# Two transformer blocks on one core: the second feed-forward begun with half of its second gate tile, kept in a place of its own, and the last input norm taken in two halves of the tokens

## What is computed

```
        x = x + rmsnorm(merged @ w_out[l], post_mix_w[l])
        h = rmsnorm(x, pre_ffn_w[l])
        f = (jax.nn.silu(h @ w_gate[l]) * (h @ w_up[l])) @ w_down[l]
        x = x + rmsnorm(f, post_ffn_w[l])
```

## Time and profile before

| | us |
|---|---|
| median of 3 runs | 2957.29 |
| lowest, highest | 2957.23, 2958.44 |
| the profiled execution, whole | 2958.75 |
| its span in the trace | 2956.9 |
| mean granted TensorE clock, as a share of 2.4 GHz | 0.991 |

### The profile page before, as it was taken

One profiled execution on the slowest core, in us unless ns is written; L12 is line 12 of the kernel. 1 busy time (PEld: TensorE's weight loads), 2 busy tenths in 40 slices (PEclk: granted clock), 3 DMA queues, 4 the chain that ended last, 5 costly groups with the idle time before them and its releaser, 6 DMA issues.

```text
span 2956.9 us, 31552 instructions
## 1 busy us (share of the span) xinstructions
PE 2868.3 (97%) x13108; PEld 2322.7 (79%) x13108; DVE 1393.5 (47%) x1660; ACT 957.4 (32%) x1255; POOL 369.7 (13%) x333
## 2 busy tenths in 40 slices
PE   8999999999999999999999999999999999999997
PEld 6877668888888888788878887667777888888886
DVE  6775544453535453633234444665564213232334
ACT  4313442321312122321246565654352222111122
POOL 1213112000000000201012222133320000000004
PEclk9999999999999999999999999999999999999998
DMA  3225523111111111245423332665531111111113
GB/s 116 79 79 137 145 65 109 49 39 61 42 52 40 61 36 54 93 142 185 162 72 98 107 93 78 192 203 167 210 118 56 41 57 39 61 36 58 43 61 118
DMA packets 88655, 270.01 MB, mean 91 GB/s; under 512 B 12600, under 2 KB 17336, under 8 KB 88512
## 3 DMA queue, kind: packets, MB, share of 16 engines
q1 hardware_dynamic: 74016, 221.61, 24.1%
q0 software_dynamic: 14496, 46.38, 4.5%
HBM read 215.35 MB, written 52.59 MB: 91 GB/s over the span
## 4 chain that ended last, share of the span: by engine, by line
PE 83%; DVE 8%; ACT 3%; issue 2%; DMA 2%; POOL 1%; DVEq 0%; SPq 0%; ACTq 0%; POOLq 0%
PE ps L211 82%; DVE cacc L182 1%; ACT PB L176 1%; PE ps L214 1%; POOL ga L179 1%; DVE PB L182 1%; DVE ps L191 1%; DVE YA L179 1%; DVE sqacc L179 1%; DVE YA L182 0%; DVE XT L179 0%; DMA xin<-in_xT 0%; DMA raw<-in_w_w2out 0%; ACT wh L176 0%; DVE AL L182 0%
## 5 line engine op out<-in xcount | busy, mean ns | idle before, releaser
L211 PE MATMUL ps<-AH,wh 128*128 128x512 f32 (+1 forms) x2232 | 887.5, 398 | 38.1 <-DVE wl L179 13.3
L211 PE MATMUL ps<-AH,wl 128*128 128x512 f32 (+1 forms) x2232 | 871.7, 391 | 0.0
L211 PE MATMUL ps<-AL,wh 128*128 128x512 f32 (+1 forms) x2232 | 871.2, 390 | 0.0
L179 DVE TENSOR_TENSOR wl<-raw,wh 128x1024 fp32r<-128x1024 f32 (+2 forms) x227 | 269.4, 1187 | 808.7 <-ACT wh L176 808.6
L211 PEld LDWEIGHTS ps<-AH,wh 128*128 128x128 f32 (+1 forms) x2232 | 418.8, 188 | 140.1 <-DVE AL L182 15.4
L176 ACT ACTIVATE wh<-raw 128x1024 fp32r<-128x1024 f32 (+2 forms) x274 | 252.5, 922 | 766.4 <-PE ps L211 754.2
L211 PEld LDWEIGHTS ps<-AH,wl 128*128 128x128 f32 (+1 forms) x2232 | 418.6, 188 | 91.1
L211 PEld LDWEIGHTS ps<-AL,wh 128*128 128x128 f32 (+1 forms) x2232 | 419.0, 188 | 88.3 <-issue 2.9
L211 PE MATMUL ps<-UH,wh 128*128 128x512 f32 (+1 forms) x840 | 325.2, 387 | 0.0
L211 PE MATMUL ps<-UL,wh 128*128 128x512 f32 (+1 forms) x840 | 325.1, 387 | 0.0
L211 PE MATMUL ps<-UH,wl 128*128 128x512 f32 (+1 forms) x840 | 325.1, 387 | 0.0
(11 more groups left out here) (219 smaller groups left out, 3209.0 us busy)
## 6 DMA issues: line engine op xcount, KB each, us to landing
raw<-in_w_up SPq DMA_DIRECT2D x44, 512.0 KB, 3.4
raw<-in_w_gu SPq DMA_DIRECT2D x44, 512.0 KB, 3.4
raw<-in_w_w2in SPq DMA_DIRECT2D x32, 512.0 KB, 4.3
raw<-in_w_down SPq DMA_DIRECT2D x48, 256.0 KB, 2.6
raw<-in_w_down SPq DMA_DIRECT2D x32, 320.0 KB, 2.8
xin<-in_xT SPq DMA_DIRECT2D x16, 512.0 KB, 4.8
stk<-scr_ka SPq DMA_DIRECT2D x32, 256.0 KB, 8.1
raw<-in_w_w2v SPq DMA_DIRECT2D x16, 512.0 KB, 3.4
```

Source lines behind the costliest of these rows:

```text
L179: return Issued(self, self.e.tensor_tensor(out, a, b, op))
L211: return Issued(self, self.e.matmul(out, l, r, start=start, stop=stop))
```

## The change

g1 is made early. Its two parts get a place of their own, slot 5 of `UH2` and `UL2`, which is free once the `w_out` product is over. The first half of g1 (bank 6) moves ahead of the second halves of g0 and u0. Norm 6 becomes two norms: 6 for the first 512 tokens, whose sums lie in u0's first half and whose rows lie in g1's first half, and 7 for the last 512, whose sums (bank 4 now) lie in g1's second half and whose rows lie in u1's first half. The sums and rows of norm 5 each move two values of k earlier. g0 and u0 are evacuated in halves (`first2`), u0's first half at the end of `dve_out2`. All later norms have a number one higher.

```diff
-    staged = [TILE["gu", ("g", 0)], TILE["gu", ("u", 0)]]
+    staged = [TILE["gu", ("g", 0)], TILE["gu", ("u", 0)], G1]
...
         elif s == staged[0]:
-            out += [(staged[0], 0), (staged[1], 0), (staged[0], 1), (staged[1], 1)]
-        elif s != staged[1]:
+            out += [(t, half) for half in range(2) for t in staged]
+        elif s not in staged:
...
     def w_halves(self, s):
+        if s == G1:
+            return self.UH2[:, 5, :], self.UL2[:, 5, :]
...
     def w_freed(self, q, s):
+        elif s == G1:
+            q.wait_ge(self.S.gem, GEM_END[TILE["w2out", (1, 7)]])
...
         def stats5(half, k):
-            if k == 6:
+            if k == 4:
                 q.wait_ge(S.pa, 21)
                 self.norm_stats(q, 5, self.acc3, 4, 8)
         def rows5(half, k):
-            if k == 2:
+            if k == 0:
                 self.norm_rows(q, 5, self.rcols[:, 12:16], 4, 8)
+            if k == 4:
+                q.wait_ge(S.xacc, 14)
+                self.norm_stats(q, 6, self.acc3, 0, 4)
+        def rows6(half, k):
+            if k == 4:
+                q.wait_ge(S.nrb, 4)
+                self.norm_rows(q, 6, self.rc8[:, 0:4], 0, 4)
...
         self.half_product(q, u0, self.Ah, self.Al, 8, 0, 2, P, None, None, True, True, rows5)
+        self.half_product(q, G1, self.Ah, self.Al, 8, 0, 6, P, None, None, True, True, rows6)
...
         x3(7, 0)
         self.norm_sqrt(q, 5, 4)
+        self.w_high(q, G1)
         rows(1)
+        self.norm_sqrt(q, 6, 4)
         for n in range(NT):
             x3(n, 1)
-        self.w_high(q, TILE["gu", ("g", 1)])
+            if n == 3:
+                q.wait_ge(S.nrow, 6)
+                q.act(self.RB[:, HALF[0]], self.bank(4), ACT.Copy).then_inc(S.nrb)
...
+    def first2(self, q, x, half):
+        q.wait_ge(self.S.gem, GEM[TILE["gu", ("g", 0)] + x, half])
+        q.wait_ge(self.S.nrb, 6 + half)
+        t = q.tt(self.cv2[2 * x][:, HALF[half]], self.bank(2 * x + half), self.RB[:, HALF[half]], ALU.mult)
+        t.then_inc(self.S.uev if half else self.S.fuh)
...
         self.w_low(q, TILE["gu", ("u", 0)])
+        self.norm_recip(q, 5, self.rcols[:, 12:16], 4)
         low(7, 0)
         total(0)
-        self.norm_recip(q, 5, self.rcols[:, 12:16], 4)
+        self.w_low(q, G1)
         mult(0, 1)
         mult(1, 1)
+        self.norm_recip(q, 6, self.rc8[:, 0:4], 4)
         add(0, 1)
...
+        self.first2(q, 1, 0)
         total(1)
-        self.w_low(q, TILE["gu", ("g", 1)])
...
+        q.wait_ge(S.nsq, 6)
+        self.half_product(q, G1, self.Ah, self.Al, 8, 1, 7, P, None, None, True, True, stats7)
+        q.wait_ge(S.fuh, 1)
+        self.half_product(q, G1 + 1, self.Ah, self.Al, 8, 0, 2, P, None, None, True, True, rows7)
+        self.f2_evac(q, 1)
+        self.half_product(q, G1 + 1, self.Ah, self.Al, 8, 1, 3)
...
         self.w_low(q, TILE["gu", ("u", 1)])
-        self.norm_recip(q, 6, self.rc8, 8)
-        evac(0)
-        evac(1)
+        self.first2(q, 0, 0)
+        self.norm_recip(q, 7, self.rc8[:, 4:8], 4)
+        self.first2(q, 0, 1)
+        self.first2(q, 1, 1)
+        gated(0)
```

More of the change, by code:

```diff
@@ L88 @@
 LAST8 = TILE["down2", (4, 0)]
+G1 = TILE["gu", ("g", 1)]
 GROUPS = [slice(0, 512), slice(512, 768), slice(768, 1024)]
@@ L481, in product, with norm_stats, norm_sqrt @@
             self.half_product(q, s, hi, lo, nk, half, 2 * pr + half, m, ready, ks, True, True, aside)
-    def norm_stats(self, q, n, acc, t0, t1):
+    def norm_stats(self, q, n, acc, t0, t1, b=7):
         for t in range(t0, t1):
-            i = q.mm(self.bank(7)[:, t - t0:t - t0 + 1], acc[:, t * 128:t * 128 + 128], self.ones[:, 0:1], True, True)
+            i = q.mm(self.bank(b)[:, t - t0:t - t0 + 1], acc[:, t * 128:t * 128 + 128], self.ones[:, 0:1], True, True)
         i.then_inc(self.S.nst)
-    def norm_sqrt(self, q, n, w):
+    def norm_sqrt(self, q, n, w, b=7):
         q.wait_ge(self.S.nst, n)
         q.wait_ge(self.S.nrc, n - 1)
-        q.act(self.scol[:, 0:w], self.bank(7)[:, 0:w], ACT.Sqrt, bias=self.epsc, scale=1.0 / 1024).then_inc(self.S.nsq)
+        q.act(self.scol[:, 0:w], self.bank(b)[:, 0:w], ACT.Sqrt, bias=self.epsc, scale=1.0 / 1024).then_inc(self.S.nsq)
     def norm_recip(self, q, n, col, w):
@@ L2846, in pe_ff2, with stats7, rows7 @@
         S = self.S
-        def norm(half, k):
-            if (half, k) == (0, 5):
+        def stats7(half, k):
+            if k == 6:
                 q.wait_ge(S.xacc, 21)
[L2851 to L2855, removed]
+                q.wait_ge(S.nrb, 6)
+                self.norm_stats(q, 7, self.acc3, 4, 8, 4)
+        def rows7(half, k):
+            if k == 2:
+                self.norm_rows(q, 7, self.rc8[:, 4:8], 4, 8)
+        q.wait_ge(S.nsq, 6)
[4 more added lines that the diff above has]
+        self.half_product(q, G1 + 1, self.Ah, self.Al, 8, 1, 3)
         for x, step in enumerate(self.STEPS2):
-            if x < 2:
+            if x < 4:
                 continue
@@ L2861, in pe_ff2 @@
             s = self.f2_tile(step)
[L2862 to L2866, removed]
+            self.f2_evac(q, x - 2)
             if isinstance(part, str):
-                self.product(q, s, self.Ah, self.Al, 8, self.f2_pair(x), P, None, None, norm if x == 2 else None)
+                self.product(q, s, self.Ah, self.Al, 8, self.f2_pair(x))
             else:
@@ L2892, in stats @@
             q.wait_ge(S.g2a, 14 + 7 * g)
-            self.norm_stats(q, 7 + g, self.acc3, GROUPS[g].start // P, GROUPS[g].stop // P)
+            self.norm_stats(q, 8 + g, self.acc3, GROUPS[g].start // P, GROUPS[g].stop // P)
         def rows(g):
-            q.wait_ge(S.nrc, 7 + g)
+            q.wait_ge(S.nrc, 8 + g)
             for t in range((GROUPS[g].stop - GROUPS[g].start) // P):
@@ L2947, in act_ff2 @@
         self.w_high(q, TILE["gu", ("u", 1)])
-        self.norm_sqrt(q, 6, 8)
-        q.wait_ge(S.nrow, 6)
-        q.act(self.RB[:, :], self.pair(2), ACT.Copy).then_inc(S.nrb)
+        self.norm_sqrt(q, 7, 4, 4)
+        q.wait_ge(S.nrow, 7)
+        q.act(self.RB[:, HALF[1]], self.bank(5), ACT.Copy).then_inc(S.nrb)
         evac(0)
@@ L2967, in act_ff2, with gated @@
             if x == 11:
-                self.norm_sqrt(q, 7, 4)
+                self.norm_sqrt(q, 8, 4)
             if x == 19:
-                self.norm_sqrt(q, 8, 2)
+                self.norm_sqrt(q, 9, 2)
             last(x)
-        self.norm_sqrt(q, 9, 2)
+        self.norm_sqrt(q, 10, 2)
     def dve_ff2(self, q):
         S = self.S
+        def gated(i):
+            cv = self.cv2[2][:, :]
+            q.wait_own()
+            q.wait_ge(S.usl, 22 + i + 1)
+            q.tt(cv, cv, self.cv2[i % 2][:, :], ALU.mult).then_inc(S.umul)
+            q.wait_ge(S.uh, 22 + i + 1)
+            q.tt(self.UL2[:, i % NU, :], cv, f32(self.UH2[:, i % NU, :]), ALU.subtract).then_inc(S.ul)
         def evac(x):
@@ L2980, in evac @@
                 q.wait_ge(S.gem, GEM[self.f2_tile(self.STEPS2[x]), 1])
-                q.wait_ge(S.nrb, 6)
+                q.wait_ge(S.nrb, 7)
                 q.wait_ge(S.umul, 22 + i - 1)
@@ L2984, in evac @@
             elif part == "u":
-                cv = self.cv2[2][:, :]
                 q.wait_ge(S.gem, GEM[self.f2_tile(self.STEPS2[x]), 1])
                 q.wait_ge(S.ul, 22 + i)
[L2988 to L2993, removed]
+                q.tt(self.cv2[2][:, :], self.pair(x % 2), self.RB[:, :], ALU.mult).then_inc(S.uev)
+                gated(i)
             elif i > 0:
@@ L3002, in scaled @@
             c = GROUPS[g]
-            q.wait_ge(S.nrow, 7 + g)
+            q.wait_ge(S.nrow, 8 + g)
             q.stt(self.YA[:, n, c], self.YA[:, n, c], self.V("postff", n), self.bank(4 + g)[:, 0:c.stop - c.start], ALU.mult,
@@ L3050, in dve_ff2 @@
             if x == 11:
-                self.norm_recip(q, 7, self.last_col(0), 4)
+                self.norm_recip(q, 8, self.last_col(0), 4)
             if 12 <= x < 16:
@@ L3057, in dve_ff2 @@
             if x == 19:
-                self.norm_recip(q, 8, self.last_col(1), 2)
+                self.norm_recip(q, 9, self.last_col(1), 2)
             if x >= 20:
@@ L3063, in dve_ff2 @@
                 squares(x)
-        self.norm_recip(q, 9, self.last_col(2), 2)
+        self.norm_recip(q, 10, self.last_col(2), 2)
         for n in range(NT):
```

## The result

| | before | changed |
|---|---|---|
| median of 5 runs, us | 2957.23 | 2945.56 |
| lowest, highest | 2951.03, 2958.44 | 2944.89, 2947.42 |
| profiled execution, us | 2958.75 | 2945.66 |
| its span | 2956.9 | 2943.9 |

The ratio of the runs is 0.9969, with a 95% interval of 0.9956 to 0.9982: faster by 5.3 to 13.0 us. One execution of the kernel before (6807 us, in E1) and one of E7 (10219 us) were slow and are left out of every ratio.

A forecast was written before the change was run, and what follows sets the result against it. The residual chain on DVE bounds the stretch, about 2.9 us per tile against 1.4 for its matmuls. u1's second half at 2240.6 instead of 2249.10 gains 8.5 us: from 2957.29 to 2948.8, range 2946.6 to 2951.9.

The forecast's parts named there:

- Units: PE prices: matmuls 0.227 us apart, four sums or rows delay the next 0.81, first matmul after a wait 0.11 longer.
- Part 1: Norm 5's sums start at 2196.61 instead of 2197.97; DVE's first `mult` starts at 2202.0, 1.36 us earlier.
- Part 2: g1's early weights lie in idle time of ACT and DVE and cost nothing; PE's 1.88 us wait for them goes.
- Part 3: DVE idles 2.0 us for norm 6 before the first `add`; the chain comes 0.82 us later, not 1.36 earlier.
- Part 4: g1's first half fills PE for 6.4 us; then waits of 0.2, 1.4 and 0.8 us at k = 4, 5, 6.
- Part 5: g1's second half follows without a wait; u1's second half starts at 2240.6 instead of 2249.10, a gain of 8.5 us.
- the margin: g1's evacuation ends at 2245.6, 0.4 us before g2 follows at 2246.1.
- The table load: Rival: Silu comes 1.3 us later, g1's evacuation ends 0.9 behind g2's due time; gain 7.6, 2949.7 us; 5%.
- The kept lead: Rival: DVE doesn't wait for norm 6, PE finds every k ready; 2.8 us more, 2946.0; 5%.
- Slipped chain: Rival: the chain on ACT and DVE costs 3 us more, reaching PE at k = 5; gain 5.5, 2951.8; 15%.
- late weights: Rival: g1's weight load lands late, holding up ACT's copy of norm 5's rows; 2963.2 us or more; 3%.
- the clock's falls: Behind the stop at 2889.62 the clock is 0.83 for 10 us, 1.7 us lost; whether it recurs was left open: ±1.7.

The follow-up runs named there:

- E1: The kernel before, executed again unaltered: median 2954.67 us against 2955.80 on the same chip, ratio 0.9995.
- E7: The kernel before without POOL's six additions of squares in the second half: stretch 50.83 us, median 2951.41 against 2955.80, ratio 0.9986.
- E5: The kernel before with only g1's weights given their own place and made early: stretch 54.93 us against 57.02, ratio 0.9990.
- E3: The changed kernel with norm 6's root and reciprocal moved behind the second residual tile: stretch 46.36 us against 48.43, median 2942.65.
- E4: The changed kernel with g1's first half put back behind the second halves of g0 and u0: stretch 54.72 us against 48.43, median 2952.28.
- E2: The changed kernel, executed again unaltered: median 2943.78 us against 2955.27 for the kernel before, ratio 0.9966, stretch 48.45 us.

## Why the prediction was right, and where it was not

- **Units.** Held: the stretch from g0's first matmul to u1's second half was forecast as 46.9 us (2240.6 less 2193.75) and came out at 46.76 and 46.79.
- **Part 1.** The sums of norm 5 start 2.90 us behind g0's first matmul (forecast 2.86), the first `mult` 8.29 (forecast 8.25).
- **Part 2.** `w_low` of g1 and its `w_high` lie in idle time; DVE still idles for 1.56 us behind it. No stop for these weights is left. E5: 2.1 us, priced at 1.88 and the restart.
- **Part 3.** DVE waits 1.92 us for norm 6 (forecast 2.0), the first `add` is 0.77 us later against g0's first matmul than before (forecast 0.82), and POOL stretches six DVE operations as before. E3: undoing this wait makes the chain 2.1 us earlier.
- **Part 4.** The waits at k = 5 and 6 are 1.23 and 0.71 of idle time; with the 0.16 by which a matmul is shown too long they are the 1.4 and 0.8 of the text. The wait of 0.2 at k = 4 came too, without a mark: 2216.34 to 2216.78 is 0.44 us where 0.227 is the usual distance, and DVE has written that `AL` at 2216.72. All three waits are as forecast.
- **Part 5 and the margin.** g1's evacuation ends at 2242.66 and g2 starts at 2243.07: 0.41 us, forecast 0.4. From there PE has no gap up to 2860. The fill is 6.3 of 8.6 us (E4); part 4 has its length at 6.4.
- **The table load.** It starts at 2234.35, right behind the copy of `RB`, and Silu 1.29 us later:

```profile
2234.35 1.28 ACT L178 ACT_TABLE_LOAD   x1
2235.64 1.06 ACT L178 ACTIVATE cv<-cv 128x1024 f32<-128x1024 f32 x1
```

  The drain of the Trainium skill (ScalarE: Activation LUTs, What ACT_TABLE_LOAD costs) does not show in this place. The rival is out; with its 1.3 us the margin of 0.41 would not have held.
- **The kept lead.** This rival's price was wrong: with the lead PE does not find every k ready. My own numbers had it: the chain of before with a lead of 1.36 has k = 6 ready at 2222.8 (2224.12 less 1.36), where PE, without a stop since 2214.0, is at 2222.2. That is a wait of 0.6 and a slower restart, and 2.1 us instead of 2.8. E3 measures 2.1, with a stop shown as 0.53 at k = 6.
- **Slipped chain, late weights.** Neither came. DVE had its six slow operations and no more, and g1's weights did not hold ACT up.
- **What was off** is the step from the stretch to the whole time. First the base: I took 8.5 off the median of three executions, 2957.29. Beside the experiments the same kernel has medians of 2955.27, 2955.80 and 2953.24 (of 21, 21 and 9 executions, on two chips); less 8.5 these give 2944.7 to 2947.3, and the measured 2945.56 lies among them. Then the scatter: I let only the clock's falls move the rest, by 1.7 us either way, but the matmuls ahead of the stretch alone end anywhere in a band of 6.8 us (2185.55 to 2192.32). The median lies 1.0 outside the range, and base and scatter are more than enough for that; the stretch, 8.6 us for a forecast of 8.5, gives no reason for it. That the medians differ by as much as 11.7 and, in E2, 11.5 us is not a success of the mechanism: the means differ by 10.5 and 9.5, and the intervals hold 8.6. Whether the whole gain is over 0.2%, which I gave 0.84, the runs don't decide: the interval of the ratio, 0.9956 to 0.9982, reaches across 0.998.

## What to carry to other kernels

Where PE waits for a chain on another engine, work for PE that needs none of that chain gains its full length if it is put ahead of the first wait and PE still waits behind it. What it needs (weights, a place for them, a bank, and a way to empty the next bank in time) has to be found first. When a small step that two in-order engines wait for is moved into such a chain, look at what stands behind it on each: here a reciprocal of 0.18 us cost 2.1. To judge a change of a few microseconds, measure the stretch between two instructions that it encloses; it repeated to 0.05 us here, while whole executions differed by several.

## What I had not expected of the hardware

- In eleven profiles of kernels whose matmuls are the same up to w_out's last one, this one starts between 2185.55 and 2192.32 us.
- A wait of PE can be real and carry no mark: 0.2 us at k = 4 shows only as a matmul of 0.50 us and a distance of 0.44.
- A stop of about the same length is followed by some 3 us at 1.2 GHz in one execution and by none in the next. Near 2118 it is 1.82 us with a fall in the first profile of the kernel before and 1.81 without one in the changed kernel's; near the end it is 1.84 with a fall (at 2889.62) and 1.92 without (at 2878.23). A fall costs some 1.6 us: 2118.01 to 2192.10 took 74.1 us with one (granted clock 0.92 from 2118 to 2140), 2116.73 to 2189.22 took 72.5 without.
